# GLA and sliding-window block in split fp32: loads, key decay, decay sums, norm spread, h scalings and token sums moved by one to four slots

## What is computed

```python
h = rmsnorm(x, g_pre)
q_a, k_a, v_a, lr_a, z_a, q_b, k_b, v_b, z_b, m_a, m_b = split(h @ w_in)
# branch A: gated linear attention, 4 heads, dk 128, dv 256, chunks of 64 tokens
log_a = log_sigmoid(lr_a @ w_decay_up + b_decay_up) / 16
for each chunk:
    b = cumsum(log_a);  k_dec = k * exp(b_last - b)
    S = S * exp(b_last) + k_dec^T v;   o = q S
y_a = (rmsnorm(o_a, g_gla) * silu(z_a)) @ w_branch_gla
# branch B: 16 query heads and 2 key heads of width 64, rotary positions,
# window of two chunks, a sink per head in the softmax
y_b = (softmax_with_sink(q k^T / 8) v * silu(z_b)) @ w_branch_swa
y   = sigmoid(m_a + b) * y_a + sigmoid(m_b + b') * y_b
out = x + rmsnorm(y @ w_out, g_post)
```

## Time and profile before

| | |
|---|---|
| median of 3 runs | 1931.96 us (1929.62 to 1933.79) |
| the profiled execution's own time | 1935.43 us |
| its span in the trace | 1933.6 us |
| PE busy | 1849.5 us, 96% |
| DVE busy | 1365.8 us, 71% |
| ACT busy | 815.3 us, 42% |
| POOL busy | 1028.3 us, 53% |
| DMA | 391.20 MB, 202 GB/s in the mean |

### The profile page before, as it was taken

One profiled execution on the slowest core, in us unless ns is written; L12 is line 12 of the kernel. 1 busy time (PEld: TensorE's weight loads), 2 busy tenths in 40 slices (PEclk: granted clock), 3 DMA queues, 4 the chain that ended last, 5 costly groups with the idle time before them and its releaser, 6 DMA issues. The chain is left out here.

```text
span 1933.6 us, 31389 instructions
## 1 busy us (share of the span) xinstructions
PE 1849.5 (96%) x11024; PEld 1472.5 (76%) x11024; DVE 1365.8 (71%) x2140; ACT 815.3 (42%) x1808; POOL 1028.3 (53%) x673
## 2 busy tenths in 40 slices
PE   8999989999999999999999999999999999999996
PEld 7877767777767777887877777777777778887885
DVE  6768866776898876747578876755988856446365
ACT  5456455433343453323257444443343453215521
POOL 5534544455444458734444555654454467538855
PEclk9999999999999999999999999999999999999998
DMA  7534376688888777886844366756778687875872
GB/s 277 135 99 134 114 209 192 172 216 231 213 223 247 222 225 250 276 275 226 236 130 146 114 166 168 177 154 161 212 228 244 203 269 230 253 234 181 279 265 109
DMA packets 474462, 391.20 MB, mean 202 GB/s; under 512 B 292835, under 2 KB 365091, under 8 KB 460995
## 3 DMA queue, kind: packets, MB, share of 16 engines
q1 hardware_dynamic: 474307, 389.20, 67.6%
HBM read 256.45 MB, written 132.64 MB: 201 GB/s over the span
## 5 line engine op out<-in xcount | busy, mean ns | idle before, releaser
L1012 PE MATMUL pu<-a_hi,w_hi 128*128 128x512 f32 x1824 | 724.1, 399 | 16.3 <-DVE u L1830 5.3
L1012 PE MATMUL pu<-a_lo,w_hi 128*128 128x512 f32 x1824 | 709.7, 392 | 0.0
L1012 PE MATMUL pu<-a_hi,w_lo 128*128 128x512 f32 x1824 | 709.0, 391 | 0.4 <-POOL w_lo L1996 0.4
L1996 POOL TENSOR_TENSOR w_lo<-t,w_hi 128x512 fp32r<-128x512 f32 x256 | 356.2, 1399 | 411.7 <-ACT w_hi L1331 411.6
L1996 POOL TENSOR_TENSOR w_lo<-w_raw,w_hi 128x512 fp32r<-128x512 f32 x264 | 402.0, 1533 | 248.4 <-ACT w_hi L1331 248.4
L1012 PEld LDWEIGHTS pu<-a_hi,w_hi 128*128 128x128 f32 x1824 | 343.8, 189 | 119.5 <-issue 44.2
L1012 PEld LDWEIGHTS pu<-a_hi,w_lo 128*128 128x128 f32 x1824 | 343.8, 189 | 74.6 <-POOL w_lo L1996 0.8
L1012 PEld LDWEIGHTS pu<-a_lo,w_hi 128*128 128x128 f32 x1824 | 344.1, 189 | 67.9
L1331 ACT ACTIVATE w_hi<-t 128x512 fp32r<-128x512 f32 x256 | 158.5, 628 | 359.1 <-DVE t L534 285.7
L1013 PE MATMUL pu<-a_hi,w_hi 128*128 128x512 f32 x544 | 213.1, 392 | 5.4 <-DVE ct L1859 5.4
L1013 PE MATMUL pu<-a_lo,w_hi 128*128 128x512 f32 x544 | 212.4, 390 | 0.0
(11 more groups left out here) (177 smaller groups left out, 2283.9 us busy)
## 6 DMA issues: line engine op xcount, KB each, us to landing
w_raw<-in_w SPq DMA_DIRECT2D x81, 1024.0 KB, 6.1
va_d<-ct SPq DMA_DIRECT2D x128, 64.0 KB
qb_d<-ct SPq DMA_DIRECT2D x32, 256.0 KB
zb_d<-ct SPq DMA_DIRECT2D x32, 256.0 KB
q_s<-qb_d SPq DMA_DIRECT2D x32, 256.0 KB, 3.8
z_s<-zb_d SPq DMA_DIRECT2D x32, 256.0 KB, 3.1
gb_d<-gb SPq DMA_DIRECT2D x32, 256.0 KB, 2.8
za_d<-ct SPq DMA_DIRECT2D x128, 64.0 KB
```

The costliest lines, as they stand in the source:

```text
L1012: return nc.tensor.matmul(dst, weights, moving, start=start, stop=stop, skip_group_check=True)
L1996: TT(flat(w_lo[o.n % NWB][:, :, :]), src, as_f32(flat(w_hi[o.n % NWB][:, :, :])), ALU.subtract) \
```

## The change

No instruction is added or removed on any engine; slots in tables and conditions move, and one call moves within SP's slot.

1. `RB`: the input norm is spread in slots 94 and 98 (before 90 and 94), waiting for one more window job (`RB_JOB` 5).
2. `HPREP`: the four h jobs begin 4 slots later. The four scalings stand one per slot in four slots (before two and two); the hx loads are one slot further ahead of the job's first slot, 99, 111, 123, 135 (before 96, 108, 120, 132); the h stores fall in slots 110, 122, 134, 146.
3. `load_gla` is issued one slot earlier, and DVE's v_g and k_g block one slot earlier, in the same slot as the state additions of the job before, and ahead of them.
4. `load_swa` (q_s, kw_s) is issued two slots earlier, except for job 0.
5. `decay_sums`, the exponential `dw` and its store come one slot later.
6. The token sums of `gb` stand one per slot in four slots (before two and two), and their store two slots later. Those of `y` stay.
7. The order of the first super-block's fills of the output stage is another: A12, A21 and S4 come first, in slots 511, 512 and 516, with their splits in 515, 517 and 520 (before 526 to 542).
8. `load_fill` stands last in SP's slot.

```diff
-        _order = (("A11", -10, -5, -6), ("A12", -9, -4, -9), ("A21", -4, 0, -9), ("A22", -3, 1, -2), ("S2", 0, 4, -5),
-                  ("S1", 1, 5, -1), ("S3", 5, 8, 6), ("S4", 6, 11, -9))
+        _order = (("A12", -20, -16, -33), ("A21", -19, -14, -33), ("S4", -15, -11, -33), ("A11", -10, -5, -6),
+                  ("A22", -4, 0, -2), ("S2", -1, 3, -5), ("S1", 0, 4, -1), ("S3", 5, 8, 6))
...
-RB = {90: 0, 94: 1}
-RB_JOB = 4
+RB = {94: 0, 98: 1}
+RB_JOB = 5
...
-HPREP = {100 + 12 * j: j for j in range(KH)}
+HPREP = {104 + 12 * j: j for j in range(KH)}
...
+SUM_STEPS = dict(gb={k: (k,) for k in range(4)}, y={0: (0, 1), 1: (2, 3)})
...
-                if r + 3 in GLA:
-                    load_gla(sb, GLA[r + 3])
+                if r + 4 in GLA:
+                    load_gla(sb, GLA[r + 4])
...
-                if r + 5 == min(SWA):
-                    load_swa(sb, 0)
-                elif r + 3 in SWA and SWA[r + 3]:
-                    load_swa(sb, SWA[r + 3])
+                if r + 5 in SWA:
+                    load_swa(sb, SWA[r + 5])
...
-                if r - 6 in DECAY:
-                    t = DECAY[r - 6]
+                if r - 7 in DECAY:
+                    t = DECAY[r - 7]
...
-                if s in fills:
-                    load_fill(fills[s])
...
-                    if s == job.first + 2:
+                    if s == job.first + len(SUM_STEPS[job.what]):
                         store_sums(job)
...
-                    if r + 4 in HPREP:
-                        j = HPREP[r + 4]
+                    if r + 5 in HPREP:
+                        j = HPREP[r + 5]
...
+                if s in fills:
+                    load_fill(fills[s])
...
-                if r - 5 in DECAY:
-                    decay_sums(NT * sb + DECAY[r - 5])
+                if r - 6 in DECAY:
+                    decay_sums(NT * sb + DECAY[r - 6])
...
-                if r in GLA:
-                    n = 16 * sb + GLA[r]
+                if r + 1 in GLA:
+                    n = 16 * sb + GLA[r + 1]
...
-                        if r in (first - 1, first):
+                        if r in range(first - 3, first + 1):
                             dve.wait_ge(hx_in, 16 * 4 * (j + 1))
                             dve.wait_ge(rb_sb_ok, 2)
-                            for o in range(2):
-                                q, k = 2 * (r - first + 1) + o, 2 * j + o
-                                STT(hx[q][:, :], hx[q][:, :], cs["gpre"][:, k:k + 1], rb[:, q // 2, :],
-                                    ALU.mult, ALU.mult).then_inc(hx_ok, 1)
+                            q = r - first + 3
+                            k = 2 * j + q % 2
+                            STT(hx[q][:, :], hx[q][:, :], cs["gpre"][:, k:k + 1], rb[:, q // 2, :],
+                                ALU.mult, ALU.mult).then_inc(hx_ok, 1)
...
-                    for k in ((0, 1), (2, 3))[s - job.first] if s - job.first in (0, 1) else ():
+                    for k in SUM_STEPS[job.what].get(s - job.first, ()):
```

More of the change, by code:

```diff
@@ L600, in load_fill @@
                     return
-                if f.name == "A11":
+                if f.name == ("A12" if (f.sb, f.what) == (0, "y") else "A11"):
                     if f.what == "gb":
@@ L1396, in _ @@
                         A(pm[2 + half][:, :], tab[:, 0, half * HT:(half + 1) * HT], ACT.Copy).then_inc(cos_ok, 1)
-                if r - 5 in DECAY:
-                    n = NT * sb + DECAY[r - 5]
+                if r - 6 in DECAY:
+                    n = NT * sb + DECAY[r - 6]
                     act.wait_ge(sf_ok, n + 1)
```

## The result

The change makes the kernel slower: 1958.2 us in the median of 4 runs (1951.5 to 1961.8), against 1932.0 before; the ratio is 1.0129, with a 95% interval of 1.0109 to 1.0149. The prediction was 1914, 18 us faster. The profiled run of the changed kernel took 1961.8 us, its span is 1960.0, 26.4 us above the span before.

What follows compares the result with a forecast made beforehand. PE, busy 96% of the span, was taken as the bound, leaving only its 84 us of standing. Terms 3.1+5.9+3.4+0+3.6+2.1 = 18.1 us gave 1914 against the median 1932.0; the 8-in-10 range ran from 1903 to 1929.

Steps and rivals of the forecast that it cites:

- slower: Rival: key block ahead of a bank's emptying in each first linear attention job, 30 us lost, 1939; chance 0.07.
- Decay sums, dw: Decay stage, one slot later: la_lo wait of 2.30 us goes but PE stands for the bank; 0, bounds 2.3 either way.
- Key block and token sums: Linear attention: key decay one slot earlier, token sums one per slot; 8.9 us won, 5.3 lost, net +3.6.
- together 1.9: Key block's price ahead of a bank's emptying: transposes 1.03 us plus product 0.86 in the median, set against each slot's margin.
- the gain of 8.9 us: Linear attention: the part of the 12.4 us of k_g waits expected to be won by earlier keys and spread sums.
- Norm spread: Input norm four slots later: of a 3.25 us wait near 316, 3.1 won before PE next needs a bank.
- h scalings: Window attention: later and one per slot, shortening the probability waits at 369.54 and 414.73; 5.9 us won, bounds 0 and 7.8.
- The rival of SP as the bottleneck of its own loads: hx loads wait for h stores, key loads behind them stay late, 3.4 us gone: 1917, within the forecast's own range.
- Key loads: Window attention, two slots earlier: of six waits, 11.5 us together, 3.4 won; bounds 0 and 11.5.
- The wait near 269: Window attention: kw_s wait of 4.65 us, expected to stay in size as one for ct; only 0.7 won.
- Fill order: Output stage: three operands split earlier, the a_lo wait of 2.11 us at 1768.54 taken whole; 2.1 won, bounds 0 and 2.1.
- Short and long blocks: Key block's length depending on GpSimd: all long (2.4 us) makes the sum 14 us, all short (1.45) 21; median taken.

Runs made afterwards that it cites:

- d_gap: Changed kernel with key block and its loads back in old slots, decay sums, dw and store one slot later for only five of eight jobs: 1929.0 us.
- u_key: Changed kernel with the key block and its loads back in the old slot, token sums still one per slot: 1938.3 us, ratio 1.0051.
- o_key: The kernel before the change, with the key block and its loads one slot early and nothing else: 1944.7 us, ratio 1.0065.
- r91_sum: r91 with the token sums two and two as before: 1925.5 us, ratio 0.9966.
- r91: Changed kernel with decay part and key block back in old slots, and DVE's 1/rms chain in slot 91 instead of 89: 1918.3 us, ratio 0.9922.
- k_behind: Changed kernel with the decay part back, and the key block one slot early but behind the PSUM bank's emptying: 1927.5 us, ratio 0.9970.

## Why the prediction was wrong

**The direction was wrong.** The forecast was a gain of 18.1 us with 0.82 on faster; it is a loss of 26. The mechanism of the rival *slower*, with 0.07, is what happened, though not in 14 of 16 jobs: four waits of 2.7 to 3.5 us in the two linear attentions were enough, and a second loss, in the decay stages, which had a bound of 2.3 us, came on top.

**Decay sums, dw: taken as 0 with 2.3 lost as the bound; 16.7 lost.** The step that failed is the bound "as much lost if dw, one slot later now, once holds the decay logits that reuse its bank for as long". I looked at the bank and DVE, and not at what stands ahead of dw on ACT: a split that waits for DVE's weight sum, and a table load of 1.28 us. The bound was taken from the wait that would go, not from the queue into which the instruction was put. It held them four times, 12.4 us in all. A wait for ct of 3 us in each stage went with the same edit; what brought it I did not take apart. The prediction's 0 for the la_lo wait was right: in d_gap most of it goes and the stage gets no shorter.

**Key block and token sums: +3.6 forecast.** u_key and o_key measure 20 and 13 us lost for the block, r91_sum 7 us won for the sums. The step that failed is the price of the block, "together 1.9" against the margin of its slot. First, the four blocks ahead of the late banks took 2.5 us and not 1.9: a GpSimd split had begun just ahead of their product. Second, the margins did not last. In u_key, with the block in its old slot, ct is ready for slot 162 only 0.14 us ahead of PE, which waited 0.46 us for it, where the margin was 1.54 before:

```profile
580.86 0.69 DVE L1842 TENSOR_TENSOR ct<-ct,pu 128x512 f32<-128x512 f32 x1
...
581.69 0.47 PE L1013 MATMUL pu<-a_hi,w_hi 128*128 128x512 f32 x1 [0.46 <-DVE ct L1842]
```

In slots 426 and 454 it is the same (1.53 and 1.15 before). I take it that in the kernel before the waits for k_g held PE back and gave DVE time, so that with these waits gone the margins go too; no run shows that by itself. In the changed kernel DVE ran without a gap from 575.84 on, a ga product ahead of the block took 1.78 us where it takes 0.68 in u_key, and slot 162 waited 3.44 us where 0.4 was forecast. And third, of the gain of 8.9 us the sums alone bring most: u_key has 3.3 us of k_g waits left out of 12.4.

**The clock.** I counted slow matmuls twice, 0.8 us at 369.54 and 0.7 at 269.64, both as a gain. PE's busy time rose 14.9 us, more than its idle time (11.5). A wait of 3.1 us costs some 6 us in slot 146. None of the losses had this factor.

**Norm spread: +3.1 forecast.** The premise that "the next thing PE needs is the bank" 3.06 us on was wrong: the chain, 4.5 us long, stayed in slot 89 and delayed the row maximum, and two slots on PE waited 3.06 us for prob. r91 moves the chain and shows what was there to win: slots 84 to 99 are 3.4 us below the kernel before, where the changed one is 1.2 above it.

**h scalings: +5.9 forecast.** The wait at 369.54 fell by 3.0 us as worked out, and slots 99 to 108 are 4.2 us shorter. The loss lies in the rest. First, the next job's first scaling waited for the hx load, whose lead the change cut from three slots to two, and 4.59 us came back at 421.56 (1.8 to 3.5 in other kernels with these h jobs). I had looked at how the load stands to the h stores ahead of it, and not at how it stands to its first use, which moved up by two slots within the job. Second, one loss was not in the sum at all: the fourth h job now runs into the linear attention, and slots 144 to 150 take 6.9 us more (3.4 to 7.4 in the table's other kernels, 0.4 to 0.6 with the h jobs as before or two slots later). The rival of SP as the bottleneck of its own loads was near this, but took the key loads for the ones that are late.

**Key loads: +3.4 forecast.** Slots 66 to 84 are 3.1 us shorter, 1.9 to 3.0 in the table's others, and kw_s isn't waited for at all. The wait near 269 came back as one for gb (2.62 at 275.37), and one of 2.49 us before the product of prob and v_s, 0.71 before, is new. No run has this term alone, and in o_key, with the old loads, these slots read -1.7 too; so that it held in size isn't shown.

**Fill order: +2.1 forecast.** The wait is 3.11 instead of 2.11 us, in r91 too. A long GpSimd split still stands just ahead of its slot, only the operand is another.

**Short and long blocks.** By the short and the long form of each block my sum would have been 21 or 14 us. Both are far off, so the choice between them was not what mattered most. The prediction left open whether GpSimd is what holds the product. The traces answer it as far as they can: all products that took over 0.46 us, before and after, began while a GpSimd instruction ran and ended 0.28 us behind its end. The length is thus no matter of two values but of how much of that instruction is left, and at the four late banks nearly all of it was. No run changes GpSimd's program alone.

## What to carry to other kernels

When an item is moved to another slot, its price is set by what stands ahead of it in its new place on its own engine and by who is behind it, not by the wait that it should remove; a value whose consumer comes one slot later needs little ahead of it in its queue. In a kernel that stands at 96% of its bounding engine, a margin that was read while another wait held that engine isn't a margin. And a costly item is best put behind the instruction for which the bounding engine waits. For the key block, behind the emptying of a bank, that alone was worth 14 us; for the chain of small instructions, behind the row maximum, 7 us in the medians, 4.8 of it read in its own slots. Two costly items in a row, like the paired sums, are better spread (7 us).

## What the hardware showed that I had not expected

A wait of 3 us costs PE more than itself, because the matmuls after it run slower: a granted clock of 0.69 over the 10 us behind such waits at 525.76 and at 587.36, and 2.9 us more for slot 146. In the five slots read in all traces the extra was 1.5 to 2.9 us behind waits of 2.7 to 4.5, and nothing behind waits up to 1.7. In k_behind the waits for ct were no longer than that.

An exponential on ACT that follows another function brought a table load of 1.28 us, between two instructions of 0.6 us, on the path of the four dw waits.

The first two instructions of DVE's chain for 1/rms, 128x8 each, took 1.24 and 1.21 us in slot 89 but 0.17 each in r91. In the changed kernel GpSimd had two splits there:

```profile
316.85 2.97 POOL L1997 TENSOR_TENSOR w_lo<-w_raw,w_hi 128x512 fp32r<-128x512 f32 x2
```

The first of the two ended at 318.57 and the second at 319.81, and DVE's two instructions ended 0.03 us behind them, at 318.60 and 319.84; in the kernel before it is the same. In r91 GpSimd ran nothing while the chain ran. It looks as if DVE had waited for GpSimd, as with k_g's product; no run changes GpSimd alone.
